# Two of GpSimd's four conditional sections move from the MLA stage into the differential attention, in pieces of 256 columns

## What is computed

```python
mod = jax.nn.silu(c) @ w_ada[l] + b_ada[l]
shift1, scale1, gate1, shift2, scale2, gate2 = jnp.split(mod, 6, axis=-1)
h = rms_norm(x, norm1_g[l]) * (1.0 + scale1[:, None, :]) + shift1[:, None, :]
z = h @ w_in[l]
c_q, c_kv, k_pe, dq, dk, dv = jnp.split(z, offsets, axis=-1)
...
mla_out = mla_attention(q_nope, q_pe, k_nope, k_pe, v_mla)
...
d_out = diff_attention(dq[..., 0, :], dq[..., 1, :], dk[..., 0, :], dk[..., 1, :], dv, lam)
...
mix = jnp.concatenate([mla_out, d_out], axis=-1) @ w_out[l]
x = x + gate1[:, None, :] * mix
h2 = rms_norm(x, norm2_g[l]) * (1.0 + scale2[:, None, :]) + shift2[:, None, :]
```

## Time and profile before

| | us |
|---|---|
| median of 3 runs | 2600.78 |
| lowest, highest | 2600.58, 2602.29 |
| the profiled execution | 2601.66 |
| its span, first to last instruction | 2600.0 |
| differential attention | 0 to 443 |
| MLA attention | 443 to 687 |
| GpSimd busy in the span | 454.9 |

### The profile page before, as it was taken

One profiled execution on the slowest core, in us unless ns is written; L12 is line 12 of the kernel. 1 busy time (PEld: TensorE's weight loads), 2 busy tenths in 40 slices (PEclk: granted clock), 3 DMA queues, 4 the chain that ended last, 5 costly groups with the idle time before them and its releaser, 6 DMA issues. The chain is left out here.

```text
span 2600.0 us, 31503 instructions
## 1 busy us (share of the span) xinstructions
PE 2374.4 (91%) x10766; PEld 1907.9 (73%) x10766; DVE 1730.8 (67%) x1998; ACT 1228.2 (47%) x1643; POOL 454.9 (17%) x396
## 2 busy tenths in 40 slices
PE   5989986899898699999999769999999999999998
PEld 4767764677576488777877558887878888888886
DVE  6378884666585799999999665445357666653344
ACT  6246764565521477676777461111553333332322
POOL 0000001887300010000000110000013332311100
PEclk7999997999897799999999879999999999999999
DMA  6131121339465799999999854343323222244453
GB/s 246 29 122 45 44 84 48 95 91 340 154 196 178 267 399 399 399 399 399 399 398 399 326 182 131 120 122 112 115 65 89 79 90 73 88 156 157 150 173 111
DMA packets 266072, 485.30 MB, mean 187 GB/s; under 512 B 19633, under 2 KB 125566, under 8 KB 265470
## 3 DMA queue, kind: packets, MB, share of 16 engines
q1 hardware_dynamic: 232734, 364.37, 40.2%
q0 software_dynamic: 26912, 98.62, 11.2%
q10 hardware_dynamic: 6336, 21.11, 2.0%
HBM read 402.25 MB, written 76.55 MB: 184 GB/s over the span
## 5 line engine op out<-in xcount | busy, mean ns | idle before, releaser
L2067 DVE TENSOR_TENSOR e_w<-e_raw,e_w 128x1024 fp32r<-128x1024 f32 x384 | 442.4, 1219 | 46.2 <-ACT e_w L2131 41.9
L2131 ACT ACTIVATE e_w<-e_raw 128x1024 fp32r<-128x1024 f32 x384 | 376.6, 1050 | 176.2 <-PE e_pgu L111 143.1
L111 PE MATMUL e_pgu<-e_w,e_xt 128*128 128x512 f32 x1536 | 369.4, 397 | 10.6 <-DVE e_w L2067 5.4
L111 PEld LDWEIGHTS e_pgu<-e_w,e_xt 128*128 128x128 f32 x1536 | 286.3, 189 | 85.4 <-DVE e_w L2067 17.8
L111 PE MATMUL s_ps<-h,s_w 128*128 128x512 f32 x1152 | 268.1, 394 | 2.1 <-DVE h L2495 2.1
L111 PEld LDWEIGHTS s_ps<-h,s_w 128*128 128x128 f32 x1152 | 218.0, 190 | 48.5 <-DVE h L2495 2.3
L111 PE MATMUL w_ps<-w_out,w_ring 128*128 128x512 f32 x1056 | 245.4, 392 | 1.9 <-DVE w_ring L3147 1.9
L111 PE MATMUL w_ps<-y 128*128 128x512 f32 x1056 | 240.1, 389 | 1.4 <-DVE w_o_full L3312 1.0
L111 PEld LDWEIGHTS w_ps<-w_out,w_ring 128*128 128x128 f32 x1056 | 199.3, 189 | 45.0 <-DVE w_out L3154 2.3
L111 PEld LDWEIGHTS w_ps<-y 128*128 128x128 f32 x1056 | 198.0, 188 | 43.4 <-issue 1.4
L111 PE MATMUL w_ps<-y,w_ring 128*128 128x512 f32 x816 | 195.9, 398 | 3.3 <-ACT w_h L2943 3.0
(11 more groups left out here) (425 smaller groups left out, 3927.9 us busy)
## 6 DMA issues: line engine op xcount, KB each, us to landing
e_raw<-in_w_expert_gate_dram SPq DMA_DIRECT2D x128, 512.0 KB, 11.3
e_raw<-in_w_expert_up_dram SPq DMA_DIRECT2D x128, 512.0 KB, 8.0
e_raw<-in_w_expert_down_dram SPq DMA_DIRECT2D x128, 512.0 KB, 10.9
w_raw<-in_ffn_w_gate_up_dram SPq DMA_DIRECT2D x48, 512.0 KB, 6.4
w_o_full<-in_ffn_w_down_dram SPq DMA_DIRECT2D x44, 512.0 KB, 4.0
y_rows<-am_zrow SPq DMA_DIRECT2D x4, 4352.0 KB, 35.9
raw_rows<-in_w_ada_dram POOLq DMA_DIRECT2D x32, 512.0 KB, 4.1
y_rows<-e_yo ACTq DMA_DIRECT2D x32, 512.0 KB, 6.3
```

The source lines that it names most:

```text
L111: o = pe.matmul(out, stat[i], mov[j], start=start and n == 0, stop=stop and n == 2)
L2067: dve.tensor_tensor(w[1][:, slot % CUT], raw[:, slot], w[0][:, slot % CUT].bitcast(F32), ALU.subtract).then_inc(low, 1)
L2131: act.activation(w[0][:, slot % CUT], raw[:, slot], ACT.Copy).then_inc(high, 1)
```

## The change

`diff_attention` gets a parameter `jobs`, the third and the fourth of the list of four (sections 4 and 5), and `mla_attention` keeps the first two. In the differential attention GpSimd works on groups of 256 columns: 4 groups for a section, 9 pieces for a group, 72 pieces in all, with two buffers of 128 x 256 and one accumulator of 128 x 256. It starts when DVE has finished the remainder of h, and afterwards issues the two loads of the latents as before. `raw` rows, `w_out` loads and all other engines' streams are unchanged.

```diff
+QUARTER = D // 4
-def diff_attention(nc, g, a, h_t, h_at):
+def diff_attention(nc, g, a, h_t, h_at, jobs):
...
+        narrow_rows = sb("narrow_rows", [P, 2, QUARTER])
+        narrow = sb("narrow", [P, QUARTER])
+        pieces = PIECE * len(jobs) * (D // QUARTER)
...
             @block.gpsimd
             def _(pool):
+                def job_of(t):
+                    u = t // PIECE
+                    w, b, cond, section, at = jobs[u // (D // QUARTER)]
+                    c0 = (u % (D // QUARTER)) * QUARTER
+                    return w, b, cond, section * D + c0, at, slice(c0, c0 + QUARTER)
+
+                def load(t):
+                    w, b, _, c0, _, _ = job_of(t)
+                    k, cols = t % PIECE, slice(c0, c0 + QUARTER)
+                    if k < KD:
+                        pool.dma_start(narrow_rows[:, t % 2, :], w[0].rearrange("(p k) n -> p k n", k=KD)[:, k, cols]).then_inc(part_in[t % 2], 16)
+                    else:
+                        pool.dma_start(narrow_rows[0:1, t % 2, :], b[0:1, cols]).then_inc(part_in[t % 2], 16)
+
+                pool.wait_ge(h_low, KD)
+                load(0)
+                load(1)
+                for t in range(pieces):
+                    u, k, row = t // PIECE, t % PIECE, narrow_rows[:, t % 2, :]
+                    _, _, cond, _, at, cols = job_of(t)
+                    pool.wait_ge(part_in[t % 2], 16 * (t // 2 + 1))
+                    if t:
+                        pool.wait_ge(step, t)
+                    if k == 0:
+                        if u:
+                            pool.wait_ge(acc_out, 16 * u)
+                        pool.tensor_scalar(narrow[:], row, cond[:, 0:1], None, ALU.mult).then_inc(step, 1)
+                    elif k < KD:
+                        pool.tensor_scalar(row, row, cond[:, k:k + 1], None, ALU.mult).then_inc(part_scaled, 1)
+                        pool.wait_ge(part_scaled, (KD - 1) * u + k)
+                        pool.tensor_tensor(narrow[:], narrow[:], row, ALU.add).then_inc(step, 1)
+                    else:
+                        pool.tensor_tensor(narrow[0:1, :], narrow[0:1, :], row[0:1, :], ALU.add).then_inc(step, 1)
+                    pool.wait_ge(step, t + 1)
+                    if t + 2 < pieces:
+                        load(t + 2)
+                    if k == KD:
+                        pool.dma_start(g.acc_dram[at][:, cols], narrow[:]).then_inc(acc_out, 16)
+                pool.wait_ge(acc_out, 16 * (pieces // PIECE))
                 pool.wait_ge(lat_out, 32)
...
-                diff_attention(nc, g, a, h_t, h_at)
+                diff_attention(nc, g, a, h_t, h_at, first_sections[2:])
...
-            mla_attention(nc, g, a, finished, first_sections)
+            mla_attention(nc, g, a, finished, first_sections[0:2])
```

More of the change, by code:

```diff
@@ L142, in diff_attention @@
                  "maxed nmax expd summed weighted combined probs turned pt_high pt_low vturned v_high v_low pv taken o_out "
-                 "lproj kproj lat_raw squared ssq rooted recip normed lat_high lat_low lat_out kpe_angle kpe_sum kpe_high kpe_low")
+                 "lproj kproj lat_raw squared ssq rooted recip normed lat_high lat_low lat_out kpe_angle kpe_sum kpe_high kpe_low "
+                 "part_in0 part_in1 part_scaled step acc_out")
         (w_in0, w_in1, w_high, w_low, w_used, proj, pj_out, swapped, cos_done, sin_done, roped, qk_high, qk_ready, scored0, scored1,
@@ L146, in diff_attention @@
          o_out, lproj, kproj, lat_raw, squared, ssq, rooted, recip, normed, lat_high, lat_low, lat_out, kpe_angle, kpe_sum, kpe_high,
-         kpe_low) = sems(nc, g, " ".join("ad_" + s for s in names.split()))
-        w_in = (w_in0, w_in1)
+         kpe_low, part_in0, part_in1, part_scaled, step, acc_out) = sems(nc, g, " ".join("ad_" + s for s in names.split()))
+        w_in, part_in = (w_in0, w_in1), (part_in0, part_in1)
         names = ("ident_in c_in lam_in rows_in rows_clear cs_in lat_w_in x_in0 x_in1 x_in2 x_in3 x_in4 x_in5 x_in6 x_in7 "
```

## The result

The changed kernel took 2605.82 us (median of 16 runs, 2600.96 to 2609.23) against 2600.99 us before (16 runs, 2595.98 to 2602.29): a ratio of 1.0020, interval 1.0013 to 1.0028, so some 5 us slower. Its profiled execution took 2609.16 us, 7.5 more than the profiled one of before, at the upper end of its runs; stage by stage it shows more than the median loss.

A forecast was written before the change was run, and what follows sets the result against it. DVE was taken to bound 113 to 162 us, TensorE 162 to 300. Terms 5.4 + 1.5 - 0.5 = +6.4 us on the profiled 2601.66 gave 2608.1, or 2607.2 against the median; range 2600.5 to 2617.

The forecast's parts named there:

- GpSimd's new work: Differential attention: multiply 0.86 and add 0.74 us, 8 groups of 25 us from 68 us, ending near 300 with blocking.
- DVE in the prologue: From 113 to 162 us, where DVE bounds: GpSimd's SBUF instructions stall DVE's two-input ones by 5.4 us, without slack.
- The 17 pieces: GpSimd's expected pieces between 113 and 162 us, 2.9 us each, blocking included, making 34 instructions.
- the 0.57 us of a hold: Average time a GpSimd multiply or add holds the port against DVE, from 0.40 us and 0.74 us.
- the half of the requests that go ahead: Of 19 GpSimd requests meeting DVE's two-input work from 113 to 162 us, half were taken to precede its next instruction.
- The multiply's 0.40 us: Time one 256-column GpSimd multiply holds the port: a quarter of 1.0 us and the fixed part.
- The lower end: From 113 to 162 us, DVE instructions only meet what is running: 26 x 0.12 = 3 us of stall.
- Heads 0 and 1: From 162 to 300 us: about 10 us more DVE work, mostly in spare time; 1.5 us lost, ends 0 and 10.
- the 24 us of DVE's spare time: From 162 to 300 us DVE is busy 114.0 of 138 us; most added work was to fall in the rest.
- MLA: Half of GpSimd's work there gone, ending near 562 instead of 677 us: -0.5 us, between 0 and -1.9.
- The third rival: MLA after 562 us: freed DVE and queues shorten TensorE's waits, gaining 3 to 6 us, 2597 us; chance 0.06.
- The second rival: Heads 0 and 1: nearly every GpSimd request goes ahead, DVE becomes the bound, 19 us lost, 2620 us; chance 0.14.

The follow-up runs named there:

- the run with multiplies alone: Changed kernel with GpSimd's adds in the differential attention replaced by memsets, multiplies kept: ratio 1.0004 (0.9995 to 1.0013) to the kernel before.
- the one with adds: Changed kernel with GpSimd's multiplies in the differential attention replaced by memsets, adds kept: ratio 1.0015 (1.0006 to 1.0024) to the kernel before.
- the empty MLA: Kernel before with all GpSimd loads and arithmetic in MLA left out, four stores of a cleared tile remaining: ratio 0.9996 (0.9987 to 1.0005).
- the run with memsets: Changed kernel with every GpSimd multiply and add in the differential attention replaced by a memset: ratio 0.9999 (0.9990 to 1.0008) to the kernel before.
- the second trace: The changed kernel run once more, unaltered, against the kernel before: ratio 1.0027 (1.0016 to 1.0038).

## Why the prediction was right, and where not

The forecast was 2607.2 us, +6.4, by DVE being held off in the prologue; measured was 2605.8, +4.8, and the mechanism is shown: the loss goes with GpSimd's reads and stays without the loads' bytes. How close the sum came is in part luck, though: 2.6 us too much in the prologue and 1.8 too little in the heads nearly cancel.

- *GpSimd's new work*: pieces of 0.86 and 0.74 us were 0.93 and 0.74, the end near 300 us was 297. The waits for the stores were 19.6 us in 7 in place of 21.
- *DVE in the prologue*, 5.4 us: 2.8 us, and 3 in the rows. Two factors of that term were too large. The 17 pieces were some 13, because GpSimd was slower than reckoned and stood still for 7.9 us of that stretch; with 13 the same working gives 4.1 us. The rest lies in the 0.57 us of a hold or in the half of the requests that go ahead. The multiply's 0.40 us is the likelier one: the run with multiplies alone cost the prologue 1.0 us, the one with adds 3.9. The lower end, 3 us, was right in size.
- *Heads 0 and 1*, 1.5 us: 3.3 us by the marks in both traces. DVE's additional work there, 4.6 us between the marks, was below half of my 10 us (the combination of the two maps took 1.36 instead of 1.285 us; I had said 1.4); but most of it reached the marks. TensorE's idle time rose by 1.8 us: beside the 2.8 us that it waits in both traces, four new waits of 0.2 to 0.6 us stand in the changed one, all of them for ScalarE. That ScalarE was late because of DVE is argued from the order of a step, not shown. Where the other 1.5 us lie, in which TensorE counts as busy, is not shown either. So the 24 us of DVE's spare time was not the cover that I took it for: it is an average, and a single step can have none. I had said so of the steps with rotation, and then priced it at 1.5.
- *MLA*, -0.5 us: +0.4 us by the marks, and the empty MLA shows nothing to gain that could be measured. The third rival (2597 us) falls: the stretch from 620 to 676 us in which TensorE idled for 11.0 us shows 6.5 in the changed trace, but it lies elsewhere in the program, and the stage is as long as before.
- *The rule of the Trainium skill* (SBUF — State Buffer, Who interferes with whom): a DVE instruction with two SBUF inputs contends with a GpSimd instruction that reads SBUF, and the ports they share are an exclusive lock. I read it as a block for the whole length of any such instruction. The adds agree (DVE's end 1.08 us after the add's). The multiplies do not: 58.8 us of them cost the prologue 1.0 us and the heads nothing, 46.7 us of adds 3.9 and 2.3. The same section says that a GpSimd instruction that only writes does not contend with a two-input one; the run with memsets agrees, 0.9999.
- *The second rival* (DVE becomes the bound, 2620 us) did not come: TensorE was busy for 133.4 of the 138.1 us and its granted clock was 0.98, as between the same marks before.

The last two marks are not fully explained. From head 2 to the first maximum of MLA the changed trace loses another 0.3 us net. In that stretch TensorE's granted clock differs: from 400 to 440 us it is 0.63 in the changed trace and 0.74 in that of before. TensorE is at the lower of its two levels (1.2 of 2.4 GHz) for more of it, in a head where it idles for a third of the time in both. In the multiply-only run the way from the last step's first maximum to MLA's first took 44.7 us, in the changed kernel 50.3, in the one before 49.6, and with the empty MLA, whose differential attention is that of before, 48.0. Which part of that is clock and which is arrival was not tried; it can move a single trace by more than the whole multiply effect, so I rest nothing under 2 us on one trace's last marks.

## What to carry to other kernels

An engine with nothing to do is not free: before giving it work, look for what it shares with the one that bounds the stage, and first try leaving its present work out altogether. Here that one run, the empty MLA, would have shown that there was nothing to gain. If GpSimd must work beside a DVE that reads two SBUF tensors, its instructions with one tensor input or none were nearly free here, and short two-input ones (0.46 us) cost less than longer ones (0.74 us); but what stands behind them on its queue must still be on time.

## What the runs showed that I had not expected

- Halving the width of GpSimd's instructions lessened the loss, although there are twice as many, an add being 0.46 against 0.74 us long: 1.5 instead of 3.3 us in the prologue with one section, and 1.4 instead of 4.6 us of additional DVE work in heads 0 and 1 with two. The totals, 1.0017 and 1.0002, have intervals that just touch. No run shows why it falls faster than the length.
- A small store of GpSimd (128 KB) kept it waiting for 7.88 us when 4 MB of SP's stores were under way, where the others took about 2; 6.9 us at the same place in the second trace.
- 9.4 us of additional DVE work in MLA cost nothing, 4.6 us in heads 0 and 1 of the differential attention cost 3.3. I take it that the slack of the single step decides, in each stage anew; no run varies that slack.
